# Layer-1 head outputs computed token-major and normalized by row sums on ScalarE, in a two-layer decoder step on Trainium2

## The reference

```
def gla_scan(q, k, v, g, s0, chunk):
    ...
    def step(state, xs):
        qc, kc, vc, gc = xs
        b = jnp.cumsum(gc, axis=2)
        o_inter = jnp.einsum('bhtd,bhde->bhte', qc * jnp.exp(b), state)
        ...
        o = o_inter + jnp.einsum('bhts,bhse->bhte', scores, vc)
        ...
        return state, o

def odd_layer(h, s0, has_meta, ...):
    ...
    o = rms_norm(o.astype(h.dtype), norm_g).reshape(B, T, GLA_VW) * jax.nn.silu(gate)
    h = h + rms_norm(o @ w_out, post_g)
    return h, st
```

## Time and profile before

| | |
|---|---|
| median of 3 runs | 2025.7 us (2025.2 to 2025.81) |
| the profiled execution, its time | 2029.64 us |
| its span, first to last instruction | 2027.7 us |
| mean granted TensorE clock | 0.975 of full speed |
| PE busy | 1961.5 us, 97% of the span |
| ACT busy | 641.9 us, 32% |
| DVE busy | 835.6 us, 41% |
| POOL busy | 689.0 us, 34% |

### The profile page before, as it was taken

The page is one execution under the profiler, slowest core; times in us unless marked ns, Lnnn a source line. Parts: engine busy times, 40 slices in busy tenths (PEclk is TensorE's granted clock), DMA queues, the critical chain, the costliest instruction groups (busy, mean ns, idle before and its releaser), DMA issues.

```text
span 2027.7 us, 38550 instructions
## 1 busy us (share of the span) xinstructions
PE 1961.5 (97%) x15065; PEld 1845.0 (91%) x15065; DVE 835.6 (41%) x1469; ACT 641.9 (32%) x1156; POOL 689.0 (34%) x304
## 2 busy tenths in 40 slices
PE   6999999999999999999899999999999999989999
PEld 6998998899889988999779989988998899879999
DVE  5366338534852676000351365054406532650003
ACT  5132223222321324222242343233324422442213
POOL 2333233233323322545314224323342333224551
PEclk8999999999999999999899999998999899979999
DMA  6554345434533453532234453434344424544232
GB/s 203 164 163 129 103 116 158 124 91 126 168 106 97 134 152 117 157 88 84 82 103 116 125 159 92 126 120 162 84 126 146 138 82 120 177 137 133 84 93 96
DMA packets 357436, 252.55 MB, mean 125 GB/s; under 512 B 15135, under 2 KB 324784, under 8 KB 356720
## 3 DMA queue, kind: packets, MB, share of 16 engines
q1 hardware_dynamic: 316194, 186.70, 32.1%
q10 hardware_dynamic: 41070, 63.46, 9.3%
HBM read 213.62 MB, written 36.96 MB: 124 GB/s over the span
## 4 chain that ended last, share of the span: by engine, by line
PE 85%; DVE 8%; issue 4%; ACT 2%; DMA 1%; POOL 0%; ACTq 0%; DVEq 0%; SPq 0%; POOLq 0%
PE proj L1003 70%; PE scratch L1003 9%; PE score L1003 3%; PE scratch L1006 2%; DVE kv L1551 1%; PE proj L1006 1%; DVE xlo L1425 1%; DVE xlo L1423 1%; DVE ek L1822 1%; DVE probw L1579 1%; DVE el L1818 0%; DVE tz L1412 0%; DVE sall L1554 0%; DMA xin<-in_x_prompt 0%; ACT ek L862 0%
## 5 line engine op out<-in xcount | busy, mean ns | idle before, releaser
L1003 PE MATMUL proj<-xhi,wlo 128*128 128x268 f32 x4096 | 1198.3, 293 | 17.2 <-DVE xlo L1425 7.5
L1003 PE MATMUL proj<-xlo,whi 128*128 128x268 f32 x4096 | 1187.1, 290 | 0.0
L1003 PE MATMUL proj<-xhi,whi 128*128 128x268 f32 x4096 | 1186.9, 290 | 0.0
L547 POOL TENSOR_TENSOR wlo<-wraw,whi 128x1024 fp32r<-128x1024 f32 x258 | 635.5, 2473 | 1101.3 <-ACT whi L613 1101.3
L1003 PEld LDWEIGHTS proj<-xhi,wlo 128*128 128x128 f32 x4096 | 787.2, 192 | 38.8 <-issue 23.1
L1003 PEld LDWEIGHTS proj<-xlo,whi 128*128 128x128 f32 x4096 | 786.5, 192 | 0.7
L1003 PEld LDWEIGHTS proj<-xhi,whi 128*128 128x128 f32 x4096 | 783.4, 191 | 0.0
L613 ACT ACTIVATE whi<-wraw 128x1024 fp32r<-128x1024 f32 x258 | 265.0, 1046 | 381.1 <-PE proj L1003 275.6
L1730 DVE TENSOR_SCALAR mix<-proj,cols 128x536 f32 x32 | 24.8, 775 | 341.2 <-ACT te L619 177.8
L1412 DVE TENSOR_TENSOR tz<-proj,rstd 128x536 f32<-128x536 f32 x72 | 51.3, 713 | 236.4 <-PE proj L1003 235.4
L728 ACT ACTIVATE probw<-score,small 128x128 f32<-128x128 f32 (+3 forms) x64 | 33.2, 523 | 173.7 <-DVE small L1502 173.7
(11 more groups left out here) (286 smaller groups left out, 1756.5 us busy)
## 6 DMA issues: line engine op xcount, KB each, us to landing
wraw<-in_w_in SPq DMA_DIRECT2D x192, 512.0 KB, 4.1
wraw<-in_w_out SPq DMA_DIRECT2D x64, 512.0 KB, 4.1
kv<-in_cache_k SPq DMA_DIRECT2D x128, 128.0 KB, 2.3
kv<-in_cache_v SPq DMA_DIRECT2D x128, 128.0 KB, 2.3
sst<-in_state_gla ACTq DMA_DIRECT2D x32, 512.0 KB, 4.9
out<-sst ACTq DMA_DIRECT2D x32, 512.0 KB, 3.5
hbuf<-h_residual ACTq DMA_DIRECT2D x2, 4288.0 KB, 14.8
vb<-v_sample_rows ACTq DMA_DIRECT2D x32, 256.0 KB, 5.5
```

The lines of the kernel that those rows point to most:

```text
L547: pool.tensor_tensor(wlo[:, slot, :, 0:width], wraw[:, kc, :, 0:width], whi[:, slot, :, 0:width].bitcast(F32), ALU.subtract).then_inc(s_lo, 1)
L1003: return pe.matmul(out, lhsT, rhs, start=start, stop=stop, skip_group_check=True)
```

## The change

The outputs of a block are computed with tokens on the partitions. For prompt block c, `token_outputs` takes `ed` (or `st`) as the stationary operand with all 512 columns of `state` (or `gv`) moving: three instructions where there were twelve. The result lies in the second half of `score`, no longer in a scratch bank. ACT (`token_rows`) then squares it with a sum along the row, takes Ln and Exp of the sum, and writes the row scaled by the norm to `orow`. One step later PE transposes `orow` in four pieces (TRc) into a scratch bank, and ACT's `o_rows` copies that to `og`. The sample outputs are one matmul of 8x512 in the middle of chunk 23 (`sample_outputs`, called by `chunk` between its two halves); TR5 follows after that chunk. SO, SS0 to SS2, the squares on ACT, the additions on POOL and DVE and the second multiplication of DVE are left out. `x_lo` of the first five tiles of the last projection is no longer interrupted by the additions.

```diff
-HEAD_LINKS = 14
-PAIR_LINKS_ACT, HEAD_LINKS_ACT = 8, 12
+HEAD_LINKS = 10
+PAIR_LINKS_ACT, HEAD_LINKS_ACT = 8, 30
...
-    16: "SK0 B0", 17: "OC0 SU00 SU01 SK1", 18: "OC1 SU10 SU11 B2 SK2",
-    19: "OC2 SU20 SU21 SK3", 20: "OC3 SU30 SU31 B4 SK4", 21: "OC4 SU40 SU41",
-    22: "B6", 23: "SO SS0 SS1 SS2",
+    16: "SK0 B0", 17: "OC0 SU00 SU01 SK1", 18: "TR0 OC1 SU10 SU11 B2 SK2",
+    19: "TR1 OC2 SU20 SU21 SK3", 20: "TR2 OC3 SU30 SU31 B4 SK4", 21: "TR3 OC4 SU40 SU41",
+    22: "TR4 B6", 23: "TR5",
...
-                    if c == 22:
-                        pool.wait_ge(s_gsq, 2 * s + 1)
-                        for x, y in ((gq[:, 0, 0:TP], gq[:, 1, 0:TP]), (gk[:, 0, 0:TP], gk[:, 1, 0:TP])):
-                            pool.tensor_tensor(x, x, y, ALU.add).then_inc(s_gadd, 1)
-                        pool.wait_ge(s_gadd, 3 * s + 2)
-                        pool.tensor_tensor(gq[:, 0, 0:TP], gq[:, 0, 0:TP], gk[:, 0, 0:TP], ALU.add).then_inc(s_gadd, 1)
...
+                def token_rows(c):
+
+                    w = P if c < TT else (TAIL if c == TT else NB)
+                    o, total, root = score[0:w, GV:2 * GV], stat[0:w, 16 + c:17 + c], stat[0:w, 24 + c:25 + c]
+                    act.wait_ge(s_otok, 6 * s + c + 1)
+                    chain.link(act.activation(orow[0:w], o, ACT.Square, accum_out=total))
+                    chain.link(act.activation(root, total, ACT.Ln, scale=1.0 / GV, bias=eps[0:w]))
+                    chain.link(act.activation(root, root, ACT.Exp, scale=-0.5))
+                    act.activation(orow[0:w], o, ACT.Copy, scale=root).then_inc(s_orow, 1)
...
                     if 17 <= c < 22:
-                        o_rows(c - 17)
+                        if c > 17:
+                            o_rows(c - 18)
                         if c < 21:
+                            act.wait_ge(s_otok, 6 * s + c - 16)
                             decay_start(c - 16)
+                        token_rows(c - 17)
                         if c < 20:
                             decays(c - 15)
                     if c == 22:
+                        o_rows(TT)
                         act.wait_ge(*free_d.at("head", "SU41", s))
                         act.dma_start(gla_prompt[0, bass.ds(s, 1)].rearrange("o (j p) v -> p (o j) v", p=P), state[:]).then_inc(s_gout, 16)
-                        act.wait_ge(s_so, 8 * s + 8)
-                        for v in range(4):
-                            last = act.activation((gq, gk)[v // 2][:, v % 2, 0:TP], og[:, v, 0:TP], ACT.Square)
-                        last.then_inc(s_gsq, 1)
+                token_rows(TT + 1)
                 if last_head:
                     x_hi("out1", 0, 2)
...
+                o_rows(TT + 1)
...
+                def token_outputs(c):
+
+                    w = P if c < TT else TAIL
+                    pe.wait_ge(*free_d.at("head", f"SK{c}", s))
+                    pe.wait_ge(*free_a.at("head", "VT13", s))
+                    if 6 * s + c:
+                        pe.wait_ge(s_orow, 6 * s + c)
+                    o = score[0:w, GV:2 * GV]
+                    if c:
+                        pe.wait_ge(*ed_ready.at("head", str(c), s))
+                        pe.wait_ge(*free_d.at("head", f"SU{c - 1}1", s))
+                        for j in range(2):
+                            matmul(o, ed[:, j, 0:w], state[:, j, :], start=j == 0, stop=False)
+                    matmul(o, st[0:w, 0:w], gv[0:w, c, :], start=c == 0, stop=True).then_inc(s_otok, 1)
+
+                def sample_outputs():
+
+                    pe.wait_ge(s_srow, s + 1)
+                    pe.wait_ge(s_orow, 6 * s + TT + 1)
+                    matmul(score[0:NB, GV:2 * GV], fold, srow).then_inc(s_otok, 1)
...
-                    elif kind == "OC":
+                    elif kind == "TR":
                         c = int(op[2])
-                        w = P if c < TT else TAIL
...
+                        w = P if c < TT else (TAIL if c == TT else NB)
+                        pe.wait_ge(s_orow, 6 * s + c + 1)
                         for v in range(4):
-                            o, vc = out[:, v * w:(v + 1) * w], slice(v * P, (v + 1) * P)
-                            if c:
-                                for j in range(2):
-                                    matmul(o, state[:, j, vc], ed[:, j, 0:w], start=j == 0, stop=False)
-                            last = matmul(o, gv[0:w, c, vc], st[0:w, 0:w], start=c == 0, stop=True)
+                            last = transpose(out[:, v * w:(v + 1) * w], orow[0:w, v * P:(v + 1) * P])
                         done(last)
...
                 for v in range(4):
-                    link(dve.scalar_tensor_tensor(out=og[:, v, :], in0=og[:, v, :], scalar=cols[:, GN + v:GN + v + 1], in1=r, op0=ALU.mult, op1=ALU.mult))
                     m = tile_at(mix, 4 * s + v)
-                    last = dve.tensor_tensor(m, m, og[:, v, :], ALU.mult)
+                    last = dve.scalar_tensor_tensor(out=m, in0=og[:, v, :], scalar=cols[:, GN + v:GN + v + 1], in1=m, op0=ALU.mult, op1=ALU.mult)
```

More of the change, by code:

```diff
@@ L100 @@
 PAIR_JOBS = [x for x in PAIR_OPS if x not in [f"S{t}{h}" for t in range(5) for h in "AB"]]
-HEAD_JOBS = [x for x in HEAD_OPS if x[0] != "B"]
+HEAD_JOBS = [x for x in HEAD_OPS if x[0] != "B" and x[:2] != "OC"]
 JOBS = {"pair": PAIR_JOBS, "head": HEAD_JOBS}
 BY_ACT = {"pair": [j for j in PAIR_JOBS if j[:2] in ("KT", "VT", "SS", "UT", "SN")],
-          "head": [j for j in HEAD_JOBS if j[:2] in ("VT", "OC", "SS")]}
+          "head": [j for j in HEAD_JOBS if j[:2] in ("VT", "TR")]}
 BY_DVE = {p: [j for j in JOBS[p] if j not in BY_ACT[p]] for p in JOBS}
@@ L372, in build @@
         og = sb1("og", [P, 4, T])
+        orow = sb1("orow", [P, GV])
         refs = sb1("refs", [P, 2, 17])
@@ L967, in head @@
                     x_hi("out1", 5, 7)
-                norm_log(2)
-                act.wait_ge(*free_a.at("head", "SS2", s))
-                act.activation(r, r, ACT.Exp, scale=-0.5).then_inc(ro_ready.sem, 1)
             with act.Fori(0, GH - 1) as s:
@@ L1006, in transpose, with chunk @@
                 return pe.transpose(out, x, ident[0:x.shape[0], 0:x.shape[0]])
-            def chunk(n, par, kc):
+            def chunk(n, par, kc, between=None):
                 if kc == 0:
@@ L1021, in chunk @@
                         last = matmul(out, whi[:, slot, k, :], xhi[:, kt, x], start=False, stop=kt == KT - 1)
+                    if a == 0 and between:
+                        between()
                 if kc == 1:
@@ L1339, in run @@
                         done(matmul(out[:, 0:GV], kd[0:w, j * P:(j + 1) * P], gv[0:w, c, :]))
-                    elif op == "SO":
-                        pe.wait_ge(s_srow, s + 1)
-                        for v in range(4):
-                            last = matmul(out[:, v * NB:(v + 1) * NB], srow[:, v * P:(v + 1) * P], fold)
-                        done(last)
-                    elif kind == "SS":
-                        lo_t, hi_t = SS_COLS[int(op[2])]
-                        if op == "SS2":
-                            pe.wait_ge(s_gadd2, 2 * s + 2)
-                        else:
-                            pe.wait_ge(s_gadd, 3 * s + 3)
-                        done(matmul(out[:, 0:hi_t - lo_t], ones, gq[:, 0, lo_t:hi_t]))
                     else:
@@ L1355, in head @@
                 for c in range(2 if s == 0 else 0, 24):
[L1356 removed]
+                    chunk(n0 + c // 2, (1 + c // 2) % 2, c % 2, sample_outputs if c == 23 else None)
                     for op in (HEAD_PLAN.get(1, "") + " " if s == 0 and c == 2 else "").split() + HEAD_PLAN.get(c, "").split():
@@ L1908, in head @@
                         dve.tensor_copy(srow, score[:, 0:GV]).then_inc(s_srow, 1)
-                    if c == 23:
-                        dve.wait_ge(*full.at("head", "SO", s))
-                        dve.wait_ge(*free_a.at("head", "OC4", s))
-                        dve.tensor_copy(og[:, :, TP:T], bank_of("head", "SO")[:, 0:4 * NB].rearrange("p (v b) -> p v b", v=4)).then_inc(s_fd, 1)
                 if last_head:
-                    x_lo("out1", 0, 2)
-                dve.wait_ge(s_gsq, 2 * s + 2)
-                dve.tensor_tensor(gq[:, :, TP:T], gq[:, :, TP:T], gk[:, :, TP:T], ALU.add).then_inc(s_gadd2, 1)
-                dve.wait_ge(s_gadd2, 2 * s + 1)
-                dve.tensor_tensor(gq[:, 0, TP:T], gq[:, 0, TP:T], gq[:, 1, TP:T], ALU.add).then_inc(s_gadd2, 1)
-                if last_head:
-                    x_lo("out1", 2, 5)
+                    x_lo("out1", 0, 5)
                 gate(3)
```

34 lines of the change are left out of this document (9 added, 25 removed).

## The result

The changed kernel takes 2003.8 us in the median (2002.5 to 2005.3) against 2025.45 us of the kernel before: a ratio of 0.9894, interval 0.9877 to 0.9911, so 21.7 us or 1.1% less. The forecast was 2013.3 us and the range 2004.0 to 2021.5; the direction was right, and the time lies just under the range, at the value that rival B gave (2004.7). In later sets the same kernel had medians of 2005.1 and 2006.0, with single runs from 2001 to 2010.

The account below looks back on a forecast made before the run. PE, busy in 97% of the span and partly at 1.2 GHz, was taken as the bound. +5.3 − 8.0 + 1.8 − 9.2 + 0.9 − 3.2 = −12.4 from 2025.7 gave 2013.3 us, range 2004 to 2021.5.

Parts of the forecast that it names:

- rival B: In block 4 and chunk 22 the clock never falls: −8.6 us against the forecast, 2004.7 us; chance 0.17.
- The fall of the clock: Block 4 and chunk 22: 17.2 us lost to the clock, half assumed to stay (+8.6), net −8.0 us.
- TR0 to TR2: Transposes after blocks in four heads, 0.44 us each on PE's path, twelve in all: +5.3 us.
- The ends of heads 0 to 2: From SO through the next head's first two chunks: removed instructions, wait and slow clock give −9.2 us.
- TR4: Transposes standing alone after chunk 22 in four heads, 0.44 us each: +1.8 us.
- the last head's sample: The sample outputs' matmul inside chunk 23 of the fourth head: +0.9 us.
- The tail: Last head's end: one DVE multiplication fewer per channel group while PE waits for `x_lo`: −3.2 us.
- The edits at nothing: ACT's `token_rows`, squares and additions, state store and queue order: hidden by idle engines or slack, costing nothing.
- A: In block 4 and chunk 22 the clock falls as much as before: +8.6 us, 2021.9 us; chance 0.19.
- C: ACT becomes the bound: `token_rows` ahead of the decays delays SK; +27 us, 2040, at a 6 us chain; chance 0.05.
- D: Transposes bring the clock down, 1.54 us at each of 16 places: +24.6 us, 2038 us; chance 0.04.
- E: PE waits ahead of TR5 for ACT, 1.35 us at three head ends: +4.1 us, 2017.4 us; chance 0.09.

Follow-up runs that it names:

- e1: The changed kernel, unaltered, timed again beside other runs: 2005.1 us, ratio 0.990 to the kernel before.
- e7: The changed kernel with ACT's square, Ln, Exp and scaled copy done twice in a row for every block: 2016.4 us, ratio 0.9955.
- e13: The changed kernel, unaltered, timed again in a later set: 2006.0 us, ratio 0.9902.
- e12: The changed kernel with a second DVE multiplication per channel group at the end of each head: 2007.8 us, ratio 0.9899.
- e6: The changed kernel with the sample's matmul behind chunk 23 instead of in its middle: 2017.2 us, ratio 0.996.
- e9: The changed kernel with block 4's gv,st product and state update over 128 rows, zeros beyond the 16 tokens: 2000.8 us, ratio 0.987.
- e14: The changed kernel with block 4's state update alone over 128 rows, zero-filled; gv,st keeps 16 rows: 2000.7 us, ratio 0.9874.
- e5: The changed kernel with each of TR0 to TR5 issued twice into the same bank: 2015.4 us, ratio 0.9948.
- e10: The kernel of e9, with DVE multiplying three of four channel groups' prompt columns before a head's last chunk ends: 2002.9 us, ratio 0.9882.
- e15: The kernel of e9 timed again in a later set: 2000.5 us, ratio 0.988.
- e11: The kernel before, with block 4's gv,st products and state update over 128 zero-filled rows, twelve small output instructions kept: 2008.4 us, ratio 0.9915.
- e2: The changed kernel with block 4's outputs computed by twelve instructions of 16 moving columns again: 2013.8 us, ratio 0.9945.

## Why the prediction was right or wrong

**The fall of the clock: mechanism right, the share that stays wrong.** "The bounds are none of the 17.2 us and all of them; ... and I take half: +8.6." This is the step that failed. In the profile of the result 1.5 us stayed, and the stretch takes 11.33 us at full clock instead of 11.07, 1.0 us more in four heads: −14.0 us came where −8.0 was forecast, 6.0 of the 9.5 us between the forecast and the result. That it was so little is in part luck. In the six profiles with this stretch unaltered the four heads exceed 11.33 us by 1.5 (the result), 3.1 (e1, e7), 4.6 (e13), 6.1 (e12) and 7.6 us (e6) together, 4.3 on average, a quarter of the 17.2. I had both suspects for what stays, the 16 rows of SU4 and the 16 stationary columns, and weighed them alike (gv,st, which keeps 16 rows too, I had left out); e9 and e14 show that the columns bring no fall, and that the state update does it, and then only at some of its places. No row that I had of the kernel before could have told the two apart.

**TR0 to TR2: priced right one by one, wrong in the step.** "12 × 0.44 = +5.3 us." A TR takes 0.44 us, and e5 shows it again. One transpose lasts 0.27 us in the trace, but the next begins 0.11 us behind it (four take 0.60 us, and the next row begins after 0.44), and it is the 0.11 that PE pays. But OC and SU became 0.11 and 0.08 us shorter in each step, and the first TR lies under a wait: in step 18 PE already waited 0.69 us for the copy to `og`, and 0.34 is left. +1.2 us was measured. "I cost the edit at nothing" gave away 0.1 us in 12 places, and the wait for the scratch bank was not in the sum. This is 4.1 us more.

**The ends of heads 0 to 2** came to −8.2 of −9.2 us: the sample's matmul also splits its chunk, which costs 0.28 us that I had not counted. **TR4** was +1.4 of +1.8 and **the last head's sample** +1.2 of +0.9.

**The tail** was −3.2 of −3.2, the path right and the exact figure luck. DVE's `x_lo` sets the end, as forecast, and the multiplications left out gave 3.0 us (from the first L1927 to the six `x_lo` 8.60 us, and 5.60 from the first L1913). But DVE also came to them 1.1 us sooner, which was not in the sum, and the clock behind PE's last wait took 0.9 back. And of the 6.0 us of the earlier trace rows only 4.1 were the last projection's.

**The edits at nothing** were nothing in this kernel: PE waits for no `orow`, and ACT's idle time ahead of the decays fell from 4.67 and 3.74 to 2.81 and 2.18 us. But the cover that I named was not the nearest edge; e7 shows it at TR5 and B6.

**The rivals.** B (the clock never falls) came nearest in the time, partly by luck: the falls that it left out and the longer stretch cost 2.6 us more than it had, and the cheaper TR0 to TR2 gave back 4.1. A did not come. C has its place in the sample states and at TR5 and not in the decays; one chain more costs 11 us (e7), where I had put the point at which the gain is gone near 4.8 us of chain; at two chains, 3.9 us, more than half of the gain was gone. D fell: with e5 for TR0 to TR2, and for TR3 with the stretches at 1.00 behind it in e9, e10, e14 and e15. E fell: there is no wait ahead of TR5, and e6 shows the half chunk that hides it. Its price was too high besides: PE's idle time at a head's end is 1.0 us in the first three heads and 2.4 in the last, not 1.35 in each.

The range ended at 2004.0 and the two errors of like sign, 6.0 and 4.1 us, together went past it by a hair; with the falls of e1 and e13 the same kernel's medians, 2005.1 and 2006.0, lie just inside. B's time had been computed with TR0 to TR2 at their full price, so that nothing in the range was left for both. One reading was wrong without bearing on the sum: block 0 has a third of the moving work of the others, not a quarter.

## What to carry to other kernels

Where PE is busy without a gap and slow, read the granted clock of that stretch and look for matmuls of few rows ahead of the fall; filling up the rows with zeros costs no PE time here and gave most of what a restructured computation gave (e11 −18 us, the change −21.7). When an edit is costed at nothing because an engine has idle time, find all readers of the engine's next pieces of work, and not the largest gap alone. And a step's new instruction is priced with the step that it lands in: what waited there before may hide it. A wait that grows is no loss by itself: look where the last one of them ends.

## What the runs showed of the hardware that was not expected

Matmuls over 16 rows bring the clock down although PE is never idle: behind the state update, 1.9 us of them, it fell at some places (e13: two stretches of four) and not at others, and with 128 rows, of which 112 are zero, the same columns at the same places leave it at 1.00 (e14, e15). Sixteen stationary columns over 128 rows do not (e9). Twelve small instructions of 16 moving columns over 128 rows do at some places (e11: two stretches of four), and with 16-row products among them and behind them they cost five times as much (17.2 us before, 3.3 in e11).

Twelve small instructions of which four work over 16 rows are slower even at full clock: in e11, where all have 128 rows, OC4 takes 2.60 us before SU4 starts, in e2, where the clock is still full then, 3.29 us (1391.60 to 1394.89).

```profile
1386.32 0.51 PE L1005 MATMUL scratch<-ed,state 128*128 128x16 f32 x4
...
1388.92 1.96 PE L1005 MATMUL scratch<-gv,kd 128*128 128x512 f32 x4
```

One and the same kernel varies by more than the first three runs showed: the kernel before took 2017.6 to 2030.9 us in 48 runs, the changed one 2001 to 2010. The profiles show a reason: which stretches hold a fall, and how long, changes from one execution to the next, also in unchanged code (most of the 4.85 us ahead of the first head). e9 and e15, with no fall in these stretches in their profiles, lie within 1998.8 and 2003.5.
